# An expert layer on one core: 128 of 512 tokens by rows fetched with indirect DMA, 384 in dense tiles

## The reference, cut to what matters

```python
def peer_ffn(h, w_q, keys1, keys2, u_tab, v_tab):
    q = jnp.einsum('bsd,de->bse', h, w_q).astype(jnp.float32).reshape(B, S, PEER_HEADS, PEER_D_KEY)
    s1 = jnp.einsum('bshd,hnd->bshn', q[..., :PEER_HALF], keys1.astype(jnp.float32))
    s2 = jnp.einsum('bshd,hnd->bshn', q[..., PEER_HALF:], keys2.astype(jnp.float32))
    v1, i1 = lax.top_k(s1, PEER_TOPK)
    v2, i2 = lax.top_k(s2, PEER_TOPK)
    cand = (v1[..., :, None] + v2[..., None, :]).reshape(B, S, PEER_HEADS, PEER_TOPK * PEER_TOPK)
    vals, c = lax.top_k(cand, PEER_TOPK)
    e1 = jnp.take_along_axis(i1, c // PEER_TOPK, axis=-1)
    e2 = jnp.take_along_axis(i2, c % PEER_TOPK, axis=-1)
    expert = e1 * PEER_N_KEYS + e2
    gate = jax.nn.softmax(vals, axis=-1)
    ...
    def block(args):
        hb, eb, gb = args
        u = u_tab[eb]
        act = jax.nn.gelu(jnp.einsum('td,ted->te', hb, u), approximate=False)
        v = v_tab[eb]
        return jnp.einsum('te,ted->td', gb * act, v)
```

## Time and profile before

| | |
|---|---|
| time, median of 3 runs | 3301.99 us (3300.59 to 3303.95) |
| span of the profiled execution | 3301.5 us, 0.5 us from that median |
| PE busy | 3222.1 us (98%) |
| DVE busy | 2194.6 us (66%) |
| POOL busy | 1835.7 us (56%) |
| ACT busy | 774.5 us (23%) |
| DMA | 391.67 MB, mean 119 GB/s |
| share of the chain that ended last | PE 83%, DVE 11% |

### The profile page before, as it was taken

How to read it: one execution, slowest core, us unless ns; L and a number is a source line. 1 busy time by engine, 2 the same in 40 slices (tenths; PEclk the granted TensorE clock), 3 DMA queues, 4 the chain that set the end, 5 groups by cost and what they waited for, 6 DMA issues and landing times.

```text
span 3301.5 us, 40234 instructions
## 1 busy us (share of the span) xinstructions
PE 3222.1 (98%) x15729; PEld 2673.4 (81%) x15729; DVE 2194.6 (66%) x3317; ACT 774.5 (23%) x1248; POOL 1835.7 (56%) x994
## 2 busy tenths in 40 slices
PE   7999999999999999999999999999999999999999
PEld 5787778887877887888888888888878888888887
DVE  7975389963336247675645888788843338888884
ACT  2142321211224122333121111255521001111110
POOL 4547367766541653012665666633346667777775
PEclk9999999999999999999999999999999999999999
DMA  3223123332320221001333444455543346556662
GB/s 134 83 65 102 58 90 96 96 96 90 109 77 26 90 83 58 14 22 37 121 102 122 137 139 139 133 209 193 214 167 110 121 151 193 186 187 200 198 197 96
DMA packets 164524, 391.67 MB, mean 119 GB/s; under 512 B 10864, under 2 KB 69488, under 8 KB 162288
## 3 DMA queue, kind: packets, MB, share of 16 engines
q1 hardware_dynamic: 73008, 262.64, 24.5%
q10 hardware_dynamic: 91328, 126.46, 11.3%
HBM read 326.14 MB, written 62.91 MB: 118 GB/s over the span
## 4 chain that ended last, share of the span: by engine, by line
PE 83%; DVE 11%; issue 2%; ACT 1%; DMA 1%; POOL 0%; DVEq 0%; SPq 0%; ACTq 0%; POOLq 0%
PE banks L1543 22%; PE banks L1545 22%; PE banks L1544 22%; PE banks L911 3%; DVE sb_sq L2256 3%; PE banks L794 1%; PE banks L378 1%; PE banks L802 1%; DVE sb_tmp L2266 1%; DVE sb_sq L2254 1%; PE banks L1605 1%; PE banks L1579 1%; PE banks L1581 1%; PE banks L1580 1%; DVE sb_zL L546 1%
## 5 line engine op out<-in xcount | busy, mean ns | idle before, releaser
L1531 POOL TENSOR_TENSOR sb_wL<-sb_raw,sb_wH 128x1024 fp32r<-128x1024 f32 x495 | 1207.7, 2440 | 1440.8 <-PE banks L1545 1388.5
L1543 PE MATMUL banks<-sb_hH,sb_wH 128*128 128x512 f32 x2040 | 820.9, 402 | 16.9 <-ACT sb_sq L1118 7.0
L1544 PE MATMUL banks<-sb_hL,sb_wH 128*128 128x512 f32 x2040 | 797.9, 391 | 0.0
L1545 PE MATMUL banks<-sb_hH,sb_wL 128*128 128x512 f32 x2040 | 797.8, 391 | 0.0
L1526 POOL TENSOR_SCALAR sb_wH<-sb_raw 128x1024 fp32r<-128x1024 f32 x495 | 644.4, 1302 | 13.2 <-DMA sb_raw<-in_weights 13.2
L1543 PEld LDWEIGHTS banks<-sb_hH,sb_wH 128*128 128x128 f32 x2040 | 385.3, 189 | 101.3 <-issue 19.7
L1545 PEld LDWEIGHTS banks<-sb_hH,sb_wL 128*128 128x128 f32 x2040 | 384.6, 189 | 81.6
L1544 PEld LDWEIGHTS banks<-sb_hL,sb_wH 128*128 128x128 f32 x2040 | 385.6, 189 | 73.8 <-issue 1.7
L1543 PE MATMUL banks<-sb_pzH,sb_wH 128*128 128x512 f32 x1024 | 398.8, 389 | 2.1 <-DVE sb_pzL L1467 2.1
L1545 PE MATMUL banks<-sb_pzH,sb_wL 128*128 128x512 f32 x1024 | 398.4, 389 | 0.0
L1544 PE MATMUL banks<-sb_pzL,sb_wH 128*128 128x512 f32 x1024 | 398.4, 389 | 0.0
(11 more groups left out here) (435 smaller groups left out, 4600.5 us busy)
## 6 DMA issues: line engine op xcount, KB each, us to landing
sb_raw<-in_weights SPq DMA_DIRECT2D x495, 512.0 KB, 3.7
gates<-sb_stage ACTq DMA_DIRECT2D x16, 2048.0 KB, 7.8
acts<-sb_sq ACTq DMA_DIRECT2D x96, 256.0 KB, 2.0
sb_Ga<-acts ACTq DMA_DIRECT2D x24, 1024.0 KB, 10.6
...
sb_xT<-acts ACTq DMA_DIRECT2D x1, 2048.0 KB, 10.2
```

The lines of the kernel that those rows point to most:

```text
L1531: nc.gpsimd.tensor_tensor(wL[:, t % LOS, :], raw[:, t % RAWS, :], wH[:, t % HIS, :].bitcast(F32), ALU.subtract).then_inc(sems("weights_lo" ...
L1543: pe.matmul(out, hi, H, start=start, stop=False)
L1544: pe.matmul(out, hi, L, start=False, stop=False)
L1545: return pe.matmul(out, lo, H, start=False, stop=stop)
```

## The change

- The first 128 tokens leave the dense path. All dense operands, tiles, gates, activations and products have 384 columns (`DENSE`, `DN`), and the gate stage has 96 steps instead of 128 (`GATE_STEPS`, `TG` 12).
- For the first 128 tokens POOL fetches rows by indirect DMA: for each of the 128 choices one fetch brings each token's row of 1024 floats, 512 KB in all, first from `u_rows`, then from `v_rows`: 256 fetches, 128 MB. Six buffers hold rows (`ROWS_HELD`). A table worked out (`ROWS_AFTER`) says behind which tile's low part POOL issues each, three tiles ahead of its place in DVE's order (`ROWS_AHEAD`).
- DVE multiplies each row of `u` by the token's features (put into PSUM by 16 matmuls, `token_rows`) and sums it into one of 128 numbers; ACT takes their Gelu, DVE multiplies by the gate, and then adds each row of `v`, weighted, to a sum in PSUM (`take_row`). 69 of these row operations come in the top-k stretch, three before each unit from the tenth on, 28 in the gate steps, 31 in the first 25 tiles of the late stage, and the 128 of `v` in the 93 tiles after them. PE turns the sum and DVE adds it to the residual near the end.
- All 16 groups of the first table come first, then all 16 of the second. 86 tiles stand beside top-k, 36 beside the gate steps (one step after every third eighth of a tile, three banks in turn), six behind them. All activations go through DRAM. The barrier between the stages is gone.
- In the expert layer ACT makes the weights' high parts, POOL the low parts alone.
- In the late stage ACT copies the activations into PSUM (`act_up`), and DVE's product and low part read it there instead of two operands in SBUF.
- Several semaphores of other stages are given shared names (`result_by_pe`, `block_moved0` and others), with the same waits as before.

```diff
-EARLY = 12
-BESIDE = (1, 1, 1, 2, 2, 2, 2, 5)
-LATE = GROUPS - EARLY
-TG = S // 32
+EARLY = GROUPS
+DENSE = slice(P, S)
+DN = S - P
+TG = DN // 32
+BESIDE = ((1, 2, 1, 2, 1, 2, 1, 7),) + 3 * ((2, 2, 3, 2, 2, 2, 3, 7),)
+TOPK_TILES = sum(map(sum, BESIDE))
+GATE_STEPS = 8 * TG
+GATE_TILES = 3 * GATE_STEPS // 8
+ROWS_HELD = 6
+ROWS_AHEAD = 3
...
+UNIT_DOTS = {u: (3 * (u - 9), 3 * (u - 9) + 3) for u in range(9, 32)}
+GATE_DOTS = [69 + 28 * i // GATE_STEPS for i in range(GATE_STEPS + 1)]
+LATE_ROWS = [97 + 31 * min(i, 23) // 23 if i < 25 else 128 + 128 * min(i - 25, 93) // 93 for i in range(121)]
...
+for _i in range(120):
+    for _o in range(LATE_ROWS[_i], LATE_ROWS[_i + 1]):
+        ROWS_AFTER[_o] = 8 * GROUPS + _i - ROWS_AHEAD
...
             for u in range(32):
                 if u + 1 < 32:
                     key_scores(u + 1)
-                for _ in range(BESIDE[u % 8]):
-                    one_tile(t0 + n, h_hi, h_lo)
+                if u == 0:
+                    token_rows()
+                for _ in range(BESIDE[u // 8][u % 8]):
+                    one_tile(t0 + n, d_hi, d_lo, DN)
                     n += 1
...
             turn_slots(3)
-            one_tile(t0 + n, h_hi, h_lo)
-            n += 1
...
-            for i in range(2 * TG):
-                one_tile(t0 + n, h_hi, h_lo, ready=lambda k: gate_products(4 * i + k // 2) if k % 2 else None)
+            for j in range(GATE_TILES):
+                one_tile(t0 + n, d_hi, d_lo, DN,
+                         ready=lambda k: gate_products((8 * j + k) // 3) if (8 * j + k) % 3 == 2 else None)
                 n += 1
-            E.arrive()
+            while n < 8 * GROUPS:
+                one_tile(t0 + n, d_hi, d_lo, DN)
+                n += 1
...
+            def weight_hi(t):
+
+                if t < TILE["peer"] + 16 * GROUPS:
+                    eng.wait_ge(sems(f"raw_in{t % RAWS}"), 16 * (t // RAWS) + 16)
+                    tile_ready(E, t - HIS)
...
+                    act.activation(wH[:, t % HIS, :], raw[:, t % RAWS, :], ACT.Copy).then_inc(sems("weights_hi"), 1)
...
+            load_acts(0, 0)
+            load_acts(0, 1)
+            while n < 8 * GROUPS - 3:
+                early_gelu(n)
+                n += 1
             for jj in range(2):
                 E.eng.wait_ge(sems(f"stage_out{jj}"), 16 * (TG // 2))
...
+            load_gates(0, 0)
+            load_gates(0, 1)
+            act_up(0)
+            act_up(1)
...
+            for m in range(8 * GROUPS + 8):
+                z, e = m // 8, m % 8
+                if z < GROUPS:
+                    E.eng.wait_ge(sems("pz_v"), m + 1)
+                    act.activation(B["pzH"][:, (z + 1) % 2, e, :], ps[2 + m % 2][:, 0:DN], ACT.Copy).then_inc(sems("pz_hi"), 1)
+                    if e % 4 == 3 and z + 1 < GROUPS:
+                        load_gates(z + 1, e // 4)
+                    if m + 2 < 8 * GROUPS:
+                        act_up(m + 2)
...
+                if z:
+                    weight_hi(t0 + m - 8 + HIS)
...
+            def take_row(o):
+
+                E.eng.wait_ge(sems(f"row_in{o % ROWS_HELD}"), 16 * (o // ROWS_HELD + 1))
+                row = rows_at[o % ROWS_HELD]
...
+                if o < P:
+                    ins = v.scalar_tensor_tensor(out=row, in0=row, scalar=1.0, in1=row_bank, op0=ALU.mult, op1=ALU.mult,
+                                                 accum_out=B["dots"][:, o:o + 1])
+                elif o == P:
+                    E.at("rows_used", P)
+                    ins = v.tensor_scalar(row_bank, row, B["row_weights"][:, 0:1], None, ALU.mult)
+                else:
+                    E.eng.wait_ge(sems("rows_used"), o)
+                    ins = v.scalar_tensor_tensor(out=row_bank, in0=row, scalar=B["row_weights"][:, o - P:o - P + 1], in1=row_bank,
+                                                 op0=ALU.mult, op1=ALU.add)
+                ins.then_inc(sems("rows_used"), 1)
...
+            for m in range(8 * GROUPS + 8):
+                z, e = m // 8, m % 8
+                if z < GROUPS:
...
+                    v.tensor_tensor(by_tg(ps[2 + m % 2][:, 0:DN]), by_tg(ps[4 + m % 2][:, 0:DN]), B["Gt"][:, :, e, :],
+                                    ALU.mult).then_inc(sems("pz_v"), 1)
+                if 1 <= m <= 8 * GROUPS:
+                    weighted_lo(m - 1)
+                if z:
+                    t = t0 + m - 8
                     tile_ready(E, t)
...
+                    empties(v.tensor_tensor(xT[:, e, DENSE], xT[:, e, DENSE], bank(t, DN), ALU.add), t)
+                if z and z < GROUPS:
+                    for o in range(LATE_ROWS[m - 8], LATE_ROWS[m - 7]):
+                        take_row(o)
...
         @block.gpsimd
         def _(pool):
-            for t in range(N_TILES):
+            first_late = TILE["peer"] + HIS
+            for t in range(first_late):
...
+            def fetch_row(o):
+
+                if o == 0:
+                    pool.wait_ge(sems("idx_ready"), 1)
+                if o >= ROWS_HELD:
+                    pool.wait_ge(sems("rows_used"), o - ROWS_HELD + 1)
+                nc.gpsimd.indirect_dma_start(
+                    out=rows_at[o % ROWS_HELD], out_offset=None, in_=a["u_rows"] if o < P else a["v_rows"],
+                    in_offset=bass.IndirectOffsetOnAxis(ap=B["idx"][:, o % P:o % P + 1], axis=0)).then_inc(
+                        sems(f"row_in{o % ROWS_HELD}"), 16)
+
+            o = 0
+            for t in range(first_late, N_TILES):
+                pool.wait_ge(sems("weights_hi"), t + 1)
+                pool.wait_ge(sems("tile_done"), t - LOS + 1)
+                nc.gpsimd.tensor_tensor(wL[:, t % LOS, :], raw[:, t % RAWS, :], wH[:, t % HIS, :].bitcast(F32),
+                                        ALU.subtract).then_inc(sems("weights_lo"), 1)
+                while o < 2 * P and ROWS_AFTER[o] <= t - TILE["peer"]:
+                    fetch_row(o)
+                    o += 1
```

More of the change, by code:

```diff
@@ L278, in build @@
+        rows_at = [B["rows"][:, n, :] for n in range(4)] + [
+            tmp[:, 2 * n:2 * n + 2, :].rearrange("p a b -> p (a b)") for n in range(2)]
+        row_bank = two[3][:].rearrange("p a b -> p (a b)")
         gates, acts = a["gates"], a["acts"]
@@ L1112, in second_act @@
-            t0 += 8 * EARLY
-            def late_gelu(n, t):
-                tile_ready(E, t)
-                E.at("pz_v", n - 3)
-                act.activation(sq[:, n % 4, :], bank(t), ACT.Gelu).then_inc(sems(f"bank_free{BANK[t]}"), 1)
-            for b in range(4):
-                E.eng.wait_ge(sems(f"spilled{b}"), 16 * 2 * EARLY)
-            late_gelu(0, t0)
-            late_gelu(1, t0 + 1)
+                E.eng.wait_ge(sems("gb_product"), i + 1)
+                if r == 0:
+                    E.at(f"stage_out{j % 2}", 16 * (j // 2))
@@ new lines, in second_act @@
+                act.activation(stage[:, :, 4 * r:4 * r + 4].rearrange("p e t -> p t e"),
+                               ps[2 + i % 3][:, :].rearrange("p (t e) -> p t e", t=4), ACT.Copy).then_inc(sems("gb_copied"), 1)
+                if r in (2, 5, 7):
+                    early_gelu(n)
+                    n += 1
+                if r == 7:
+                    E.eng.wait_ge(sems("gb_copied"), i + 1)
+                    eng.dma_start(gates[j].rearrange("p e t -> p (e t)"), stage.rearrange("p e t -> p (e t)")).then_inc(
+                        sems(f"stage_out{j % 2}"), 16)
@@ L1160, in second_act @@
-            load_gates(0, 1)
-            for i in range(EARLY):
-                for e in range(8):
-                    E.eng.wait_ge(sems("pz_v"), 8 * (LATE + i) + e + 1)
-                    act.activation(B["pzH"][:, (i + 1) % 2, e, :], tmp[:, e % 4, :], ACT.Copy).then_inc(sems("pz_hi"), 1)
-                    if i + 1 < EARLY and e % 4 == 3:
-                        load_gates(i + 1, e // 4)
-                        load_acts(i + 1, e // 4)
+            load_gates(0, 0)
+            load_gates(0, 1)
@@ L1496, in second_dve @@
-            for z in range(EARLY + 1):
-                early_group(z - 1, z if z < EARLY else None)
+                to = B["eg"][:, 2] if tb else B["row_gates"][:]
+                ins = v.tensor_tensor(to.rearrange("p (h s) -> p h s", h=8), cvs,
+                                      B["eg"][:, 3, 16:24].unsqueeze(2).to_broadcast([P, 8, 16]), ALU.mult)
+                if tb:
+                    ins.then_inc(sems("tk_expert"), 1)
+                else:
+                    chain(ins)
+            E.eng.wait_ge(sems("slots_copied"), 9)
@@ new lines, in second_dve @@
+            for i in range(GATE_STEPS):
+                r = i % 4
+                at = lambda c, x: B["slots"][:, c, 4 * i + x:4 * i + x + 1]
+                E.at("gb_product", i - 3)
+                v.tensor_tensor(B["onehot"][:, r], iota.unsqueeze(1).to_broadcast(bc),
+                                B["slots"][:, 0, 4 * i:4 * i + 4].unsqueeze(2).to_broadcast(bc), ALU.is_equal)
+                for x in range(4):
```

(6 more changed lines are left out.)

316 lines of the change are left out of this document (155 added, 161 removed).

## The result

The changed kernel takes 3071.07 us (median; 3069.34 to 3079.04 in 4 runs) against 3302.97 for the kernel before in the same session (3300.59 to 3305.59, 4 runs): ratio 0.9302, 95% interval 0.9289 to 0.9315. The profiled execution is the longest of the four: 3079.04 us, span 3077.3. Some 8 us of that lie ahead of the expert layer, which starts at 1766.6, not 1758.6: between 220 and 260 us TensorE is granted 0.74 of its full clock (1.00 in the kernel before), with nothing there changed. The layer itself takes 1310.7 us.

The account below looks back on a forecast made before the run. PE's matmul columns were taken to bound the kernel before, DVE top-k after the change. The expert layer's 408 + 4 + 237 + 25 + 18 + 617 + 4 = 1313 us, against 1543, gave 3072 us, range 3030 to 3115.

Parts of the forecast that it names:

- Search, 408 and 4: Top-k stretch: DVE becomes the bound at 408 us, plus 4 us for copies and the first one-hot step.
- PE at 378: Top-k stretch: PE's 86 tiles, key-score pairs and transposing products take 378 us, against DVE's 408.
- Gates, 237: Gate stage: 96 steps of 2.47 us, 237 us, with DVE's step staying beneath by 0.1.
- Six tiles and 18 us: Between gates and second table: six tiles take 25 us, then the change of stages 18, between 5 and 30.
- First 25 tiles, 115: Start of the late stage: 25 tiles with fewer rows at 4.6 us each, 115 us.
- Late loop, 93 at 4.95: Late stage from step 25: 93 tiles at 4.95 us each, 460 us.
- both limits meet: Late loop: POOL's chain at about 4.8 us and DMA at 4.5 to 5.1 us a tile, so 4.95 taken.
- DMA as the bound: Late stage: random rows lower the full DMA rate to 300 GB/s, 5.5 us a tile, 3135 us; chance 0.12.
- a fetch of 2 or 3 us: POOL's row fetch costs 2 us (3145 us, chance 0.12) or 3 us, making POOL the bound (3314 us, chance 0.05).
- rival 3: Late loop: a fetch costs 0.3 us, the loop falls beneath DMA's 4.5 us a tile, 3025 us; chance 0.12.
- Where it was freed a step before, 4.15: Late loop: if DVE freed the row buffer a step earlier, a tile takes 4.15 us.
- the last ten tiles and the tail: End of the late stage: ten tiles at 4.15 us, 42 us, and a tail of 4 us.

Follow-up runs that it names:

- e10: Changed kernel, with VectorE multiplying only the first 256 of 1024 columns in the search's 69 first-table rows (part of the reference's work left out): 3068.2 us.
- e7: Changed kernel, with three first-table tiles moved from behind the gates to the search and the first activations loaded before the gates: 3072.0 us.
- e1: Changed kernel, with rows fetched two tiles ahead instead of three (ROWS_AHEAD 2): 2995.0 us.
- e2: Changed kernel, with late-stage gates and activations loaded for the first group only and reused (part of the reference's work left out): 3064.6 us.

## Why the prediction was right, point by point

- **Matmul of 384 columns, 0.173 us**: measured 0.173.
- **The row prices**: fetch 0.95 (1.0 forecast), row sum 1.284 (1.27), dot 1.217 and 0.083 for reading the accumulator (1.27; that extra had no row), product, low part and addition 0.560, 0.549, 0.555 (0.55), high part on ScalarE 1.057 (1.06). All stood.
- **Search, 408 and 4**: 410.2. The number held, its reason only in part. VectorE's chain was sized well, 405 against 408, and it hardly waited for PE (0.5 us), as the forecast's sign for it said; at its end it waited 4.4 us for the turned slots, the forecast's 4. The step that failed is the one beside it, PE at 378 and so 30 us beneath: that term had no waits in it. With them and the low clock it is about 407. So VectorE didn't take PE's place as the bound but came to stand beside it: with 42 us of VectorE's busy time gone the search kept 404.4 (e10), and three more tiles cost 9.4 (e7). The waits I named, PE's for the key scores' banks, are not among the waits of the stage; PE waited for low parts, which POOL made late behind a fetch that waited for indices and beside VectorE's long operations. That PE's stalls came out just small enough to leave the number standing was luck.
- **Gates, 237**: 235.5, and PE busy in all of the 230 us shown. That three gate banks cost nothing held too.
- **Six tiles and 18 us**: 25 + 18 = 43; the last gate product to the second tile of the next table took 47.6, which holds one tile of that table more, so 43.4. But the parts were 33.0 up to the first tile of the second table, not 25, and 14.6 for that tile. In the 33.0 PE waited 1.6 us for a Gelu and, ahead of that first tile, 5.4 us for a low part. Issues on ScalarE's queue had idled that engine for 5.8 and 5.1 us, and its Gelus and high parts with it. The gates alone would have held PE there nearly as long, since the tile's first operand was ready only 0.15 us before the low part.
- **First 25 tiles, 115**: 128.6; 10 of the difference belong to the first of them, above. The others are 4.75 on average against 4.6.
- **Late loop, 93 at 4.95**: 457.5 us at 4.92. The chain was the forecast's, link by link. Its sum gave 9.4 us round and 4.8 a tile, and I went to 4.95 since "both limits meet"; that step was wrong, and that it met the measurement was luck. The transfers are no limit at 4.9: e1 moves the same bytes at 4.28. What the sum lacked is the time between the links: with a single row the round took 9.91 us, of which 0.28 are from the row's end to the fetch and 4.47, not 4.15, from the first matmul to the addition.
- **Rivals**: DMA as the bound is excluded by e2; a fetch of 2 or 3 us occurs only beside VectorE's long operations; one at 0.3 didn't. The loop, though, need not have stood at all: at two tiles of lead it is spread over three and lies under PE's tile. My figure for what its removal gives, 3025 by rival 3 (its own product of 42 us less gives 3030), took DMA's 4.5 as the next limit; e1 gives 2995, 30 us less. "Where it was freed a step before, 4.15" was in my text and was the lever.
- **Chances**: those listed add up to 0.95; the rest was given to nothing.

The sum, 1313 against 1310.7, is right with errors of both signs under it: search 2 and gates 1.5 too long, change about even, first 25 some 3 too short once the first is set apart, late 2.5 too long, the last ten tiles and the tail 45.7 against 46.
